# Expert stage of a hybrid encoder layer: two row buffers and two result buffers in place of three and one

## What is computed

```
expert_id = g_idx[:, None] * EXPERTS_PER_GROUP + e_idx          # 2 experts of each token
def expert_step(acc, args):
    wg, wu, wd, cw = args
    hh = jax.nn.silu(x @ wg) * (x @ wu)
    return acc + (hh * cw[:, None].astype(hh.dtype)) @ wd, None
```

## Time and profile before

| | us |
|---|---|
| three timed executions | 1353.79, 1365.91, 1362.36 |
| their median | 1362.36 |
| the profiled execution | 1353.79 |
| its span, first to last instruction | 1351.7 |
| steps of `experts` (first transposition to last write of `y`) | 941.1 to 1291.5 |
| `finish` | 1302.3 to 1348.3 |

### The profile page before, as it was taken

The page is one execution under the profiler, slowest core; times in us unless marked ns, Lnnn a source line. Parts: engine busy times, 40 slices in busy tenths (PEclk is TensorE's granted clock), DMA queues, the critical chain, the costliest instruction groups (busy, mean ns, idle before and its releaser), DMA issues. The chain is left out here.

```text
span 1351.7 us, 19893 instructions
## 1 busy us (share of the span) xinstructions
PE 1160.4 (86%) x7175; PEld 767.6 (57%) x7175; DVE 518.5 (38%) x1320; ACT 342.2 (25%) x854; POOL 295.2 (22%) x233
## 2 busy tenths in 40 slices
PE   3688999999999999999886999941989999899846
PEld 1447888888888888888673545421333333333312
DVE  2432244444444444545533466653112111111218
ACT  4422233333333333333442212210101111110102
POOL 2031313030302120110002556533112122221001
PEclk8687999999999999999998999975999999999968
DMA  9771202020202131210130111106998989999546
GB/s 374 296 279 49 77 12 89 1 89 1 69 1 75 48 89 33 67 41 32 40 147 3 61 62 47 55 24 242 424 421 319 380 359 369 392 374 370 221 183 251
DMA packets 53538, 218.56 MB, mean 162 GB/s; under 512 B 9904, under 2 KB 26680, under 8 KB 42560
## 3 DMA queue, kind: packets, MB, share of 16 engines
q1 hardware_dynamic: 36912, 117.26, 23.7%
q10 hardware_dynamic: 7632, 82.05, 15.2%
q0 software_dynamic: 8896, 17.93, 3.5%
HBM read 196.62 MB, written 30.03 MB: 168 GB/s over the span
## 5 line engine op out<-in xcount | busy, mean ns | idle before, releaser
L729 PE MATMUL att_piece_ps<-hT_hi,w_hi 128*128 128x384 f32 (+1 forms) x528 | 185.2, 351 | 2.0 <-DVE att_k_lo_sb L857 0.8
L1595 PE MATMUL moe_gu_ps<-moe_a_gu_sb,moe_xT_sb 128*64 x416 | 184.6, 597 | 2.3 <-DVE moe_xT_sb L1739 2.0
L1598 PE MATMUL moe_gu_ps<-moe_b_gu_sb,moe_xT_sb 128*64 128x512 f32 x416 | 184.6, 597 | 0.0
L729 PE MATMUL att_piece_ps<-hT_hi,w_lo 128*128 128x384 f32 (+1 forms) x528 | 173.5, 329 | 0.0
L729 PE MATMUL att_piece_ps<-hT_lo,w_hi 128*128 128x384 f32 (+1 forms) x528 | 173.1, 328 | 0.0
L916 DVE COPY att_pT_sb<-att_pT_ps 128x512 f32<-128x512 f32 (+2 forms) x192 | 94.5, 520 | 134.0 <-PE att_pT_ps L790 133.4
L1200 PE MATMUL mix_y_ps<-mix_w_out_sb,mix_oT_sb 128*128 128x512 f32 (+1 forms) x288 | 127.3, 600 | 2.2 <-ACT mix_oT_sb L1268 2.2
L1595 PEld LDWEIGHTS moe_gu_ps<-moe_a_gu_sb,moe_xT_sb 128*64 128x64 f32 x416 | 57.0, 138 | 122.0 <-issue 122.0
L977 ACT ACTIVATE att_probs_sb<-att_probs_sb,att_nmax_sb 128x640 f32<-128x640 f32 (+5 forms) x144 | 101.2, 703 | 42.1 <-DVE att_nmax_sb L902 41.3
L902 DVE CUSTOM_DVE_ANT_0 att_probs_sb<-att_s_ps,att_bias_sb 128x640 f32<-128x640 f32 (+5 forms) x144 | 95.2, 662 | 26.8 <-PE att_s_ps L778 14.6
L729 PEld LDWEIGHTS att_piece_ps<-hT_hi,w_hi 128*128 128x128 f32 x528 | 99.7, 189 | 9.3 <-issue 4.7
(11 more groups left out here) (280 smaller groups left out, 1798.9 us busy)
## 6 DMA issues: line engine op xcount, KB each, us to landing
moe_b_gu_sb<-in_w_gu ACTq DMA_DIRECT2D x26, 2048.0 KB
moe_b_dn_sb<-in_w_dn ACTq DMA_DIRECT2D x26, 1024.0 KB
moe_a_gu_sb<-in_w_gu SPq DMA_DIRECT2D x10, 2048.0 KB
keep_rows_all_sb<-in_w_ada SPq DMA_DIRECT2D x8, 2048.0 KB, 12.1
att_w_raw_sb<-in_w_qkv SPq DMA_DIRECT2D x21, 512.0 KB, 3.3
moe_a_dn_sb<-in_w_dn SPq DMA_DIRECT2D x10, 1024.0 KB
in_w_ada_sb<-in_w_ada SPq DMA_DIRECT2D x4, 2048.0 KB, 11.5
in_x_sb<-in_x_prompt SPq DMA_DIRECT2D x8, 512.0 KB, 6.8
```

What stands on the lines that cost most here:

```text
L729: ins = pe.matmul(bank[:, 0:hi - lo], w[:, kind, kc, :], x[:, kc, lo:hi], start=(m == 0), stop=(m == 3 * NC - 1))
L1595: pe.matmul(gu_ps[p % 2][LANE[0], :], xT[:, c, LANE[0]], a_gu[:, bass.ds(slot, 1), c, :].rearrange("p a n -> p (a n)"), start=(c == 0), st ...
L1598: ins = pe.matmul(gu_ps[p % 2][LANE[1], :], xT[:, c, LANE[1]], b_gu[p % 3][:, c, :], start=(c == 0), stop=(c == NC - 1))
```

## The change

`x` (the gathered rows) has two buffers in place of three, and `y` (the results) two in place of one, so the SBUF taken is the same. `y[p % 2]` waits for the scatter of step p - 2 in place of p - 1, on a semaphore of its own for each buffer. GpSimd issues `gather(p + 3)` where it issued `gather(p + 4)`: the gather that follows the scatter of step p on q0 is that of step p + 4, where it was that of p + 5. At the start it issues two listings and two gathers, then reads the number of rounds; `gather(2)` waits for `transpose_x(0)`. `SURE` is gone: all rounds but the first run under a branch. ACT issues the weights of B for step 1 before it waits for the first transposed rows, where it issued them after.

The diff, cut to its core:

```diff
-SURE = (2 * TOK // P + 1) // 2
...
-                x=[route.sb(f"x{j}", [P, D]) for j in range(3)])
+                x=[route.sb(f"x{j}", [P, D]) for j in range(2)])
...
-    y = s.sb("y", [P, D])
+    y = [s.sb(f"y{j}", [P, D]) for j in range(2)]
...
-    gathered, scattered = [s.sem(f"gathered{j}") for j in range(3)], s.sem("scattered")
+    gathered, scattered = ([s.sem(f"{n}{j}") for j in range(2)] for n in ("gathered", "scattered"))
...
-            if u < SURE:
-                body(2 * u, n)
-                body(2 * u + 1, n)
+            if u == 0:
+                body(0, n)
+                body(1, n)
...
-        if p // 2 < SURE:
+        if p // 2 == 0:
             do()
...
-        for p in range(3):
-            listing(p)
-        for p in range(3):
+        listing(0)
+        listing(1)
+        gather(0)
+        gather(1)
+        n = look(pool, T_ROUNDS, 0, 1, ROUNDS)
+        for p in range(2, 6):
+            following(pool, p, n, lambda: listing(p))
+
+        def third():
+            pool.wait_ge(xT_ready, 1)
+            gather(2)
+            following(pool, 6, n, lambda: listing(6))
+
+        following(pool, 2, n, third)
+
+        def gather_ahead(p):
+            pool.wait_ge(xT_ready, p - 1)
             gather(p)
-        for p in range(3, 6):
-            listing(p)
-        n = look(pool, T_ROUNDS, 0, 1, ROUNDS)
-
-        def gather_ahead(p):
-            pool.wait_ge(xT_ready, p - 2)
-            gather(p)
-
-        gather_ahead(3)
-        listing(6)
 
         def body(p, n):
-            following(pool, p + 4, n, lambda: gather_ahead(p + 4))
+            following(pool, p + 3, n, lambda: gather_ahead(p + 3))
...
         held = [expert(p) for p in range(3)]
-        load_gu(0, held[0])
-        load_dn(0, held[0])
-        move_xT(0)
-        for p in range(1, 2):
+        for p in range(2):
             load_gu(p, held[p])
             load_dn(p, held[p])
+        move_xT(0)
...
-            if p:
-                act.wait_ge(scattered, 16 * p)
-            act.activation(y[:, 0:512], y_ps[:, 0:512], ACT.Copy, scale=entry[:, p, 2:3].bitcast(F32))\
+            if p >= 2:
+                act.wait_ge(scattered[p % 2], 16 * (p // 2))
+            act.activation(y[p % 2][:, 0:512], y_ps[:, 0:512], ACT.Copy, scale=entry[:, p, 2:3].bitcast(F32))\
                .then_inc(y_out_act, 1)
```

More of the change, by code:

```diff
@@ L1136, in _ @@
         pool.memset(before[:, :], 0.0).then_inc(zeroed, 1)
-        for j in range(3):
+        for j in range(2):
             pool.memset(route["x"][j][:, :], 0.0).then_inc(x_zeroed, 1)
@@ L1166, in _ @@
         pool.wait_ge(listed, 32 * (NT + 1))
-        pool.wait_ge(x_zeroed, 3)
+        pool.wait_ge(x_zeroed, 2)
     @block.tensor
@@ L1549, in gather @@
             pool.wait_ge(listed[p % 4], 16 * (p // 4 + 1))
-            pool.indirect_dma_start(x[p % 3][:, :], None, k["h2"], bass.IndirectOffsetOnAxis(ap=entry[:, p, 0:1], axis=0),
-                                    bounds_check=TOK - 1, oob_is_err=False).then_inc(gathered[p % 3], 16)
-        for p in range(3):
-            listing(p)
-        for p in range(3):
-            gather(p)
-        for p in range(3, 6):
-            listing(p)
-        n = look(pool, T_ROUNDS, 0, 1, ROUNDS)
-        def gather_ahead(p):
-            pool.wait_ge(xT_ready, p - 2)
-            gather(p)
-        gather_ahead(3)
-        listing(6)
+            pool.indirect_dma_start(x[p % 2][:, :], None, k["h2"], bass.IndirectOffsetOnAxis(ap=entry[:, p, 0:1], axis=0),
+                                    bounds_check=TOK - 1, oob_is_err=False).then_inc(gathered[p % 2], 16)
+        listing(0)
[12 more added lines that the diff above has]
+            pool.wait_ge(xT_ready, p - 1)
+            gather(p)
         def body(p, n):
-            following(pool, p + 4, n, lambda: gather_ahead(p + 4))
+            following(pool, p + 3, n, lambda: gather_ahead(p + 3))
             pool.wait_ge(y_out_act, p + 1)
             pool.wait_ge(y_out_dve, p + 1)
-            pool.indirect_dma_start(k["yrows"], bass.IndirectOffsetOnAxis(ap=entry[:, p, 1:2], axis=0), y[:, :], None,
-                                    bounds_check=2 * TOK - 1, oob_is_err=False).then_inc(scattered, 16)
+            pool.indirect_dma_start(k["yrows"], bass.IndirectOffsetOnAxis(ap=entry[:, p, 1:2], axis=0), y[p % 2][:, :], None,
+                                    bounds_check=2 * TOK - 1, oob_is_err=False).then_inc(scattered[p % 2], 16)
             following(pool, p + 7, n, lambda: listing(p + 7))
         in_rounds(pool, n, body)
-        alone(pool, scattered, 32 * n, waited)
+        alone(pool, scattered[0], 16 * n, waited)
+        alone(pool, scattered[1], 16 * n, waited)
     @block.tensor
@@ L1581, in transpose_x @@
         def transpose_x(p):
-            pe.wait_ge(gathered[p % 3], 16 * (p // 3 + 1))
+            pe.wait_ge(gathered[p % 2], 16 * (p // 2 + 1))
             for c in range(NC):
-                ins = pe.transpose(xT_ps[:, c, :], x[p % 3][:, c * P:(c + 1) * P], ident)
+                ins = pe.transpose(xT_ps[:, c, :], x[p % 2][:, c * P:(c + 1) * P], ident)
             ins.then_inc(xT_ready, 1)
@@ L1640, in body @@
             elif p + 1 < STEPS:
-                if p // 2 + 1 < SURE:
+                with pe.If(n > p // 2 + 1):
                     gate_up(p + 1)
@@ L1644, in body @@
                     transpose_x(p + 2)
[L1645 to L1651, removed]
+                with pe.Else():
+                    transpose_hidden(p)
             else:
@@ L1753, in body @@
             dve.wait_ge(y_ready, p + 1)
-            if p:
-                dve.wait_ge(scattered, 16 * p)
-            dve.tensor_scalar(y[:, 512:1024], y_ps[:, 512:1024], entry[:, p, 2:3].bitcast(F32), None, ALU.mult)\
+            if p >= 2:
+                dve.wait_ge(scattered[p % 2], 16 * (p // 2))
+            dve.tensor_scalar(y[p % 2][:, 512:1024], y_ps[:, 512:1024], entry[:, p, 2:3].bitcast(F32), None, ALU.mult)\
                .then_inc(y_out_dve, 1)
```

## The result

| | before | after |
|---|---|---|
| median, us (20 runs each) | 1362.59 | 1370.13 |
| lowest to highest | 1353.79 to 1367.85 | 1362.44 to 1374.83 |
| the profiled execution | 1353.79 | 1370.43 |
| its span | 1351.7 | 1368.6 |
| transposition of the hidden rows, step 0 to step 24 | 316.3 | 331.1 |

The ratio is 1.0056 [1.0038, 1.0074]: slower by 0.56%, 7.6 us between the medians, where 12 us faster was forecast. It is a loss of less than the 1% that the prediction took as what a measurement can tell from no change, but the interval excludes no change.

The account below looks back on a forecast made before the run. PE's wait for the gate product, behind the late scatter, was taken as the bound in the expert stage. -35.8 + 6 + 12 + 5 + 1 = -12 us from 1353.8 gives 1342, placed at 1346; range 1324 to 1374.

Parts of the forecast that it names:

- 24 steps without loss: Expert stage, step 0 to step 24: 24 periods of 11.69 us make 280.6 in place of 316.3, so 35.8 us could go.
- waits in the first steps: PE at the transposition of gathered rows, at the start: gathers late beside the first weight loads, 6 us lost.
- waits beside the six loads of A: PE at the transposition of gathered rows: late gathers cost 2 us beside each of six 3.15 MB weight loads, 12 us.
- low clock: PE in the expert stage: three waits of over 2 us each cost a half-clock spell of 1.7 us, 5 us.
- first gather later: Start: B's weights of step 1, issued earlier, run beside the first gather and delay it by 1 us.
- half of that gap: Whole kernel: about half of the 8.6 us between the profiled execution and its median, added to 1342 to give 1346 us.
- the budget of 17.1 us: Queue q0 at a period of 11.69 us: the longest L may be without PE waiting for a gather.
- The branches: Expert stage, rounds made conditional: cost 0, as gate_up covers silu; without the cover some 0.3 us a step, 7 us.
- L: Queue q0: time from a scatter's issue to the landing of the gather behind it; read as 11.9, 16.2 and above 20.6 us.
- B: Rival, chance 0.20: PE waits for gathers at transpose_x in place of the scatter; 17 us slower, 1371, or 1375 with half-gap.
- A: Rival, chance 0.22: gathers always in time, DMA engines the bound; gain 24 to 28 us, 1328, or 1332 with half-gap.
- C: Rival, chance 0.08 together with a later start: the scatter wait stays, as two scatters in flight slow each other; 1354 to 1362.

Follow-up runs that it names:

- the edges alone: The kernel before with only all rounds but the first conditional and B's weights of step 1 issued before the first transposition: 1360.84 us, ratio 0.9993.
- the first experiment: The changed kernel with each gather issued ahead of the scatter of the same step in place of behind it: 1334.75 us, ratio 0.9788.

## Why the prediction was wrong

By its terms, against the profiled execution after:

| term | predicted, us | after, us |
|---|---|---|
| 24 steps without loss | 280.6 | 280.6 |
| waits in the first steps (967.68, 993.12, 1021.08) | 6 | 2.3 + 0.4 + 4.1 = 6.8 |
| waits beside the six loads of A | 6 x 2 = 12 | 25.0 |
| low clock (after: what the other rows leave) | 3 x 1.7 = 5 | 18.7 |
| first gather later | 1 | 0.1 (3.3 with the router's stage) |

These terms make the profiled execution some 17 us longer, where 12 us less was forecast. By the medians it is 7.6 us, as the profiled execution before was a fast one. The prediction allowed for half of that gap.

**What held.** The scatter's wait went, and the gate's with it. The step of 11.69 us, the budget of 17.1 us and the place of the new wait (the transposition of gathered rows, in the first steps and beside each load of A) are as derived. The branches cost nothing that the edges alone would show.

**What came out by luck.** The start was put at 6 us and has 6.8, but not by the cause given, a slow first scatter with an L of over 20.6. That L is 17.6 (975.48 to 993.12), a wait of 0.4. The 2.3 us come from elsewhere: the third gather waits 9.85 us on GpSimd for a listing that stands behind two gathers. And the 4.1 us at 1021.08 follow the load of A at 998.86 and are one of the seven waits of that kind.

The Trainium skill's page "DMA: Bandwidth & Descriptors" says in the section "Issuing engines are not separate DMA queues" that DMAs of all engines interleave on the same 16. The small loads of A agree with it: SyncE's loads made shorter take the waits for GpSimd's gathers from 31.8 us to 1.8.

**What failed: the size of L beside a load of A.** The prediction took 2 us a load, L about 19, between 16.2 as traced and 20.6. The runs show 21.1 to 21.7, a wait of 3.8 to 4.5. The 16.2 was read where the load had been issued at 1115.00 and the scatter at 1120.90. There the scatter waited for the scatter before it, and the load was already 5.9 us old. With the scatter's wait gone, y, the scatter and the load of A all start on the same event, 0.84 us apart (1051.74 and 1052.58), so scatter, listing and gather run beside the load from its start. The prediction moved the scatter in time and kept the neighbour that the old moment had given it. Holding the loads back is worth 10 us, of waits and low clock together, so the moment is part of the miss. For the rest the faster pace, which the prediction named, is the likely cause (418 GB/s beside the load of A); no run tests it by itself.

**What failed with it: the low clock.** Three spells of 1.7 us were counted. Taken step by step (the time of a step less 11.7 and less its wait), each of the seven long waits is followed by a loss of 1.7 to 3.0 us, 2.4 in the mean, and the wait of 2.31 in step 0 by 1.7. So the number was wrong above all, eight in place of three, and the price was low too. This term misses by as much as the first, 14 us against 13. With its low clock a wait of PE of about 4 us costs 5.6 to 7.4 us here; the most is the step of 19.10, 11.70 + 4.42 + 3.0.

**The rivals.** B, with a chance of 0.20, came nearest: slower, with the gather in the scatter's place. Its signs (waits of over 40 us, a clock below 0.95) came in part: 31.8 us and 0.94. Its price, 17 us slower, took a wait in every second step; the long ones come in seven steps of 24, with a larger L, and the light steps show none. That the profiled executions differ by 16.6 us, close to this price, is chance; the medians differ by 7.6. A, the DMA bound, with a chance of 0.22, did not come with this change; the first experiment comes near it: 28 us faster, with a DMA share of 0.96 in the stage. The sign that the prediction gave for itself, a DMA share above 0.95 from 1014 on, did not come: it is 0.88, less than the 0.92 before. From step 0 to step 24 the engines are busy for about as long as before (0.87 x 331.2 = 288 and 0.92 x 316.3 = 291 us), only spread over a longer time. C is excluded, as the scatter's wait is gone.

**What stays open.** How much of L's 21.4 us is the moment of the load and how much the pace. Why the profiled execution before is 8.8 us faster than its median. A kernel with three x and two y, which would give both transfers slack, was not run; it needs 4096 bytes more in each partition than either kernel. Nor was one with three x, one y and the gather first.

## What to carry to other kernels

A buffer taken from one transfer to give to another moves the wait, and the two may stand in one queue: when the slack moves, the order of issues must move with it, and here that was worth 35 us where the buffers alone cost 8. When a wait goes, ask which other transfers start on the same event as what it held back; a latency that was read at the old moment doesn't hold at the new one. And price a wait of TensorE with the low clock that follows it.

## What was not expected of the hardware

One core's DMA engines moved 418 GB/s over 20 us, with a share of 1.01, while three queues were at work. Packets, MB and share by queue, from 1054 to 1074.3 us:

```profile
q10 hardware_dynamic: 450, 4.63, 54.9%
q1 hardware_dynamic: 280, 3.01, 35.0%
q0 software_dynamic: 393, 0.81, 10.5%
```

The indirect transfers get a tenth of the engines' time beside two streams of weights. The view of the gathered rows after has this:

```profile
DMA to landing us min/median/max: 8.8/14.9/19.8
```

The same kind of transfer, 0.5 MB at most, takes from 8.8 to 19.8 us from its issue to its landing, 14.9 in the median. In this time a scatter and a listing are mostly ahead of it on q0. By the rule of the Trainium skill's page "DMA: Bandwidth & Descriptors", section "Anatomy of one DMA" (2.0 us and the bytes over 436 GB/s), a gather alone would take about 3 us, an estimate. No gather here came near that, so the rule gives no latency for a gather that stands in a queue and shares the engines with weights; which of the two costs how much, no run tells apart.
